# Head and tail of a two-layer decoder kernel: input rows loaded ahead of constants and page tables, output rows transposed straight from the residual

## What is computed

```python
def layer_prompt(x, p):
    xn = rmsnorm(x, p['norm1_g'])
    qa, ka, va, logf, glu, qc, kvc, gc, ud, vd = project(xn, pos, p)
    # four mixers: forgetting attention, convolution, sparse attention, gating
    y = merge_and_ffn(x, (o_a, o_b, o_c, o_d), p)   # h = x + o @ w_out;  y = h + relu(norm(h) @ w_ff1)^2 @ w_ff2
```

## Time and profile before

| | us |
|---|---|
| median of 3 runs | 3554.17 (3553.68 to 3555.39) |
| the profiled execution's own time | 3539.97 |
| its span in the trace | 3538.2 |
| TensorE busy in the span | 3287.5 (93%) |
| VectorE busy | 1470.2 (42%) |
| ScalarE busy | 1022.0 (29%) |
| GpSimd busy | 206.4 (6%) |

### The profile page before, as it was taken

One profiled execution on the slowest core, in us unless ns is written; L12 is line 12 of the kernel. 1 busy time (PEld: TensorE's weight loads), 2 busy tenths in 40 slices (PEclk: granted clock), 3 DMA queues, 4 the chain that ended last, 5 costly groups with the idle time before them and its releaser, 6 DMA issues.

```text
span 3538.2 us, 55597 instructions
## 1 busy us (share of the span) xinstructions
PE 3287.5 (93%) x22450; PEld 1873.5 (53%) x22450; DVE 1470.2 (42%) x2767; ACT 1022.0 (29%) x1814; POOL 206.4 (6%) x136
## 2 busy tenths in 40 slices
PE   5999988888699999999989998888887999999998
PEld 3555566666554444444445555666664444444444
DVE  4875553333544311332168566433336533113321
ACT  2112344444433310231102233444443322012211
POOL 0211110000200000000002111000001000000000
PEclk8999999999899999999999999999998999999999
DMA  6432254142221221123153325334323112111322
GB/s 197 152 103 77 75 167 141 68 144 79 81 92 42 59 60 30 42 59 91 49 145 104 103 77 151 110 91 140 122 62 103 48 48 61 47 35 47 84 73 75
DMA packets 377363, 312.49 MB, mean 88 GB/s; under 512 B 123357, under 2 KB 360314, under 8 KB 370042
## 3 DMA queue, kind: packets, MB, share of 16 engines
q1 hardware_dynamic: 369738, 208.60, 20.9%
q0 software_dynamic: 7424, 101.19, 7.7%
HBM read 264.35 MB, written 50.46 MB: 89 GB/s over the span
## 4 chain that ended last, share of the span: by engine, by line
PE 84%; DVE 6%; ACT 4%; issue 2%; DMA 2%; SPq 1%; POOL 0%; POOLq 0%; DVEq 0%; ACTq 0%
PE PS L938 44%; PE PS L1053 10%; PE PS L1313 5%; PE PS L1336 5%; PE PS L967 4%; PE PS L1204 3%; PE PS L1028 2%; PE PS L1355 1%; PE PS L1386 1%; ACT arena L1620 1%; DVE arena L1904 1%; PE PS L1250 1%; PE PS L1211 1%; DVE arena L2182 1%; PE PS L1103 1%
## 5 line engine op out<-in xcount | busy, mean ns | idle before, releaser
L938 PE MATMUL PS<-arena 128*128 128x512 bf16 (+1 forms) x10080 | 1549.1, 317 | 0.0
L938 PEld LDWEIGHTS PS<-arena 128*128 128x128 bf16 x10080 | 753.5, 98 | 794.6
L1053 PE MATMUL PS<-arena 128*128 128x512 f32 (+3 forms) x1152 | 477.6, 570 | 0.0
L1497 ACT ACTIVATE arena<-arena 128x1024 bf16<-128x1024 f32 (+1 forms) x112 | 145.4, 1300 | 1097.0 <-PE PS L938 1076.9
L2481 DVE TENSOR_TENSOR arena<-PS,arena 128x1088 f32<-128x1088 f32 (+1 forms) x48 | 62.0, 1292 | 654.8 <-PE PS L938 631.2
L1053 PEld LDWEIGHTS PS<-arena 128*128 128x128 f32 (+1 forms) x1152 | 208.6, 184 | 236.3 <-issue 203.3
L2187 DVE TENSOR_REDUCE arena<-PS 128x1 f32<-128x1024 f32 (+5 forms) x192 | 138.9, 724 | 362.3 <-PE PS L1316 361.6
L1313 PE MATMUL PS<-arena 128*128 128x512 f32 (+3 forms) x576 | 231.1, 509 | 8.0 <-ACT arena L1629 8.0
L2505 DVE SCALAR_TENSOR_TENSOR arena<-PS,arena 128x1088 f32<-128x1088 f32 x64 | 82.7, 1292 | 354.7 <-PE PS L938 354.3
L1336 PE MATMUL PS<-arena 128*128 128x64 f32 x1632 | 213.4, 276 | 0.0
L1336 PEld LDWEIGHTS PS<-arena 128*128 128x128 f32 x1632 | 201.1, 195 | 8.2 <-issue 5.2
(11 more groups left out here) (340 smaller groups left out, 2871.1 us busy)
## 6 DMA issues: line engine op xcount, KB each, us to landing
arena<-in_w_ff SPq DMA_DIRECT2D x64, 512.0 KB, 4.1
arena<-in_w_ff SPq DMA_DIRECT2D x32, 1024.0 KB, 5.9
arena<-in_cache_nsa_kv SPq DMA_DIRECT2D x256, 64.0 KB
x_s<-arena SPq DMA_DIRECT2D x24, 544.0 KB, 3.5
arena<-x_s SPq DMA_DIRECT2D x2, 4352.0 KB, 13.0
arena<-in_w_in SPq DMA_DIRECT2D x4, 2048.0 KB, 14.7
arena<-in_w_out SPq DMA_DIRECT2D x16, 512.0 KB, 4.3
arena<-in_w_in SPq DMA_DIRECT2D x12, 512.0 KB, 5.7
```

Source lines behind the costliest of these rows:

```text
L938: last = mm(PS[:, 1536 * k + a:1536 * k + a + wd], ww[:, c, :], xx[:, c, a:a + wd], start=c == 0 and n == 0, stop=c == blocks - 1 and n == 2)
L1053: last = mm(PS[0:r, c * 512:c * 512 + b - a], XNT[:, j, t * P:t * P + r], Wt[:, j, a:b], start=j == 0, stop=j == KD - 1)
L1497: run(WH[k][:, 0:blocks, :], src[k][:, 0:blocks, :], ACT.Copy).then_inc(S["w_hi"], 1)
```

## The change

SyncE now issues the identity alone, then row tiles 0 to 2, then the rest of the constants, then tiles 3 to 8, each into a buffer of its own, with no waits. After them come the page-table loads: `pages`, four loads that write `piece_rows` straight from the page table (one for every fourth partition; `quad_s` is gone), and the 16 of `block_rows`. Gains and gate weights follow, then the wait for the last copy, and the barrier; the eight stores of the residual are issued after the barrier, ahead of the layer's loads. TensorE waits for the identity alone before it starts. VectorE works out the page rows between the sums of tiles 6 and 7. In the tail TensorE transposes straight out of `XT` and uses all eight banks (four tiles), ScalarE copies the first half of each tile and VectorE the second, and each tile has its own buffer `XS`, so that no wait for a store is left before the end.

```diff
-        XS = [lo.take(DM) for _ in range(2)]
-        XO = [lo.take(KD * P, k=KD, n=P) for _ in range(2)]
+        XS = [lo.take(DM) for _ in range(QT + 1)]
...
         def _(sp):
-            sp.dma_start(const, A["consts"]).then_inc(loaded_once, 16)
+            sp.dma_start(const[:, 0:P], A["consts"][:, 0:P]).then_inc(ident_in, 16)
...
+            for t in range(3):
+                row_in(t)
+            sp.dma_start(const[:, P:], A["consts"][:, P:]).then_inc(const_in, 16)
+            for t in range(3, QT + 1):
+                row_in(t)
             sp.dma_start(pages, A["page_table"].rearrange("b j -> (b j)").unsqueeze(0)).then_inc(loaded_once, 16)
-
+            for r in range(4):
+                sp.dma_start(piece_rows[r:P:4, 0:4], A["page_table"].rearrange("b j -> (b j)").rearrange("(g n) -> n g", g=4)).then_inc(loaded_once, 16)
             for j in range(NPG):
                 r = slice(j * (P // NPG), (j + 1) * (P // NPG))
                 sp.dma_start(block_rows[r, :], A["page_table"][:, j:j + 1].rearrange("b o -> o b").to_broadcast([P // NPG, NB])).then_inc(loaded_once, 16)
-            sp.dma_start(quad_s.unsqueeze(2), A["page_table"].rearrange("b j -> (b j)").unsqueeze(1).to_broadcast([NB * NPG, 4]).unsqueeze(2)).then_inc(quad_out, 16)
-            sp.wait_ge(quad_out, 16)
-            sp.dma_start(piece_rows[:, 0:4], quad_s.rearrange("(g n) r -> (n r) g", g=4)).then_inc(loaded_once, 16)
...
             sp.wait_ge(S["row_ev"], QT + 1)
+            arrive(sp, "sp")
             for n in range(KD):
                 store_residual(n)
-            arrive(sp, "sp")
...
-            pe.wait_ge(loaded_once, 304)
...
+            pe.wait_ge(ident_in, 16)
+            for t in range(QT + 1):
+                k, r = t % 2, rows_of(t)
+                pe.wait_ge(S[f"row_in{t}"], 16)
+                if t >= 2:
                     pe.wait_ge(S["row_ev"], t - 1)
                 for j in range(KD):
                     at = (2 * k + j // 4) * 512 + (j % 4) * P
-                    last = tr(PS[:, at:at + r], XS[k][0:r, j * P:(j + 1) * P], ident[0:r, 0:r])
+                    last = tr(PS[:, at:at + r], XS[t][0:r, j * P:(j + 1) * P], ident[0:r, 0:r])
...
+            pe.wait_ge(const_in, 16)
             arrive(pe, "pe")
...
-            def row_out(t, k, m):
+            for t in range(QT + 1):
                 r = rows_of(t)
-                pe.wait_ge(S["row_cp"], t + 1)
-                if not (isinstance(t, int) and t < 2):
-                    pe.wait_ge(S["row_ev"], t - 1)
+                if t >= 4:
+                    pe.wait_ge(S["row_ev"], t - 3)
+                    pe.wait_ge(S["row_odd"], t - 3)
                 for j in range(KD):
-                    at = (2 * k + j // 4) * 512 + (j % 4) * P
-                    last = tr(PS[0:r, at:at + P], XO[k][:, j, 0:r], ident)
+                    at = (2 * (t % 4) + j // 4) * 512 + (j % 4) * P
+                    last = tr(PS[0:r, at:at + P], XT[:, j, t * P:t * P + r], ident)
...
-                if not (isinstance(t, int) and t < 2):
-                    act.wait_ge(S[f"row_out{k}"], 16 * m)
-                run(XS[k][0:r, 0:512], PS[0:r, 1024 * k:1024 * k + 512], ACT.Copy)
-                run(XS[k][0:r, 512:1024], PS[0:r, 1024 * k + 512:1024 * k + 1024], ACT.Copy).then_inc(S["row_ev"], 1)
...
+                run(XS[t][0:r, 0:512], PS[0:r, at:at + 512], ACT.Copy).then_inc(S["row_ev"], 1)
...
-            dve.wait_ge(loaded_once, 304)
+            dve.wait_ge(ident_in, 16)
+            dve.wait_ge(const_in, 16)
...
+            def page_rows():
+
+                dve.wait_ge(loaded_once, 336)
...
+            for t in range(QT + 1):
+                if t == QT - 1:
+                    page_rows()
+                row_squares(t, t % 2, t // 2)
             arrive(dve, "dve")
...
-            def row_cp(t, k, m):
-                r = rows_of(t)
-                if not (isinstance(t, int) and t < 2):
-                    dve.wait_ge(S["row_T"], t - 1)
-                V.tensor_copy(XO[k][:, :, 0:r], XT[:, :, cols(t)]).then_inc(S["row_cp"], 1)
...
+            for t in range(QT + 1):
+                r, at = rows_of(t), t % 4 * 1024 + 512
+                dve.wait_ge(S["row_T"], t + 1)
+                V.tensor_copy(XS[t][0:r, 512:DM], PS[0:r, at:at + 512]).then_inc(S["row_odd"], 1)
...
-            pool.wait_ge(loaded_once, 304)
+            pool.wait_ge(loaded_once, 336)
```

More of the change, by code:

```diff
@@ L172, in build_step @@
         y_s = scratch("y_s", (P, 2 * ROWS))
-        quad_s = nc.dram_tensor("quad_s", (NB * NPG, 4), I32).ap()
         x_s = scratch("x_s", (P, KD * ROWS))
@@ L428, in build_step @@
         loaded_once = sem("loaded_once")
-        quad_out = sem("quad_out")
+        ident_in = sem("ident_in")
+        const_in = sem("const_in")
         names("act_done dve_done")
-        names("col_inv col_mean col_rstd row_mean row_rstd row_in0 row_in1 row_T row_ev row_out0 row_out1 row_cp")
+        names("col_inv col_mean col_rstd row_mean row_rstd row_in0 row_in1 row_in2 row_in3 row_in4 row_in5 row_in6 row_in7 row_in8 row_T row_ev row_odd row_out")
         names("sq_ready sq_added sq_summed xn_ready xt_free w_tok gains glu_mm glu_ev glu_in glu_sig glu_done")
@@ L436, in build_step @@
         names("x_in head_in v_in0 v_in1 gate_in kv4_in fox_ready sl_in snb_in rank_ready rank_out q_in aux_in ocb_in os_out oc_ready sm_ready ce2 dmx dex ee_ready wt_ready vb_ready s_mm nm_ready p_ready pt_T pt_evA pt_evD pv_mm o_done cs_ready ce_ready cp_ready o_ready o_out pad_ready")
[L437 removed]
+        names("od_in oh_in gn_in yb_in wo_in od_norm ss_ready h3_sq oa_hi u_hi oa_ready oa_T oa_ev y_hi")
         names("g2_in xh_ready xl_ready w_in0 w_in1 w_hi w_lo g_mm g_ev u_ready")
@@ L510, in arrive @@
             e.sem_clear(go[who])
[L512 to L533, removed]
         SUMS_OF = {3: [(1, 0), (1, 1)], 4: [(1, 2), (2, 0)], 5: [(2, 1), (2, 2)], 6: [(3, 0), (3, 1)], 7: [(3, 2)]}
@@ L589, in _, with row_in @@
         def _(sp):
-            sp.dma_start(const, A["consts"]).then_inc(loaded_once, 16)
+            sp.dma_start(const[:, 0:P], A["consts"][:, 0:P]).then_inc(ident_in, 16)
+            def row_in(t):
+                src = A["x_prompt"][0, t * P:(t + 1) * P, :] if t < QT else A["x_sample"].rearrange("b t d -> (b t) d")
+                sp.dma_start(XS[t][0:P if t < QT else NS, :], src).then_inc(S[f"row_in{t}"], 16)
+            for t in range(3):
[3 more added lines that the diff above has]
+                row_in(t)
             sp.dma_start(pages, A["page_table"].rearrange("b j -> (b j)").unsqueeze(0)).then_inc(loaded_once, 16)
+            for r in range(4):
+                sp.dma_start(piece_rows[r:P:4, 0:4], A["page_table"].rearrange("b j -> (b j)").rearrange("(g n) -> n g", g=4)).then_inc(loaded_once, 16)
             for j in range(NPG):
@@ L620, in _ @@
             first = slice(0, 1)
-            over_tiles(sp, row_in, between={5: lambda: (norm_in(first), gates_in(0, first))})
-            gates_in(1, first)
+            norm_in(first)
+            for f in range(2):
+                gates_in(f, first)
             def store_residual(n):
@@ L881, in _ @@
                 arrive(sp, "sp")
-            def row_out(t, k, m):
+            for t in range(QT + 1):
+                dst = O["y_prompt"][0, t * P:(t + 1) * P, :] if t < QT else O["y_sample"].rearrange("b t d -> (b t) d")
                 sp.wait_ge(S["row_ev"], t + 1)
[L886 to L893, removed]
+                sp.wait_ge(S["row_odd"], t + 1)
+                sp.dma_start(dst, XS[t][0:P if t < QT else NS, :]).then_inc(S["row_out"], 16)
             for f in range(2):
@@ L897, in _ @@
             sp.wait_ge(x_out, 128 * (layers + 1))
-            sp.wait_ge(S["row_out0"], 16 * 5)
-            sp.wait_ge(S["row_out1"], 16 * 4)
+            sp.wait_ge(S["row_out"], 16 * (QT + 1))
         @block.tensor
@@ L1787, in _ @@
                 arrive(act, "act")
-            def row_out(t, k, m):
-                r = rows_of(t)
+            for t in range(QT + 1):
+                r, at = rows_of(t), t % 4 * 1024
                 act.wait_ge(S["row_T"], t + 1)
-                if not (isinstance(t, int) and t < 2):
-                    act.wait_ge(S[f"row_out{k}"], 16 * m)
-                run(XS[k][0:r, 0:512], PS[0:r, 1024 * k:1024 * k + 512], ACT.Copy)
-                run(XS[k][0:r, 512:1024], PS[0:r, 1024 * k + 512:1024 * k + 1024], ACT.Copy).then_inc(S["row_ev"], 1)
-            over_tiles(act, row_out)
+                run(XS[t][0:r, 0:512], PS[0:r, at:at + 512], ACT.Copy).then_inc(S["row_ev"], 1)
         @block.vector
@@ L1814, in _ @@
             V.tensor_copy(wnegb, C("wneg"))
[L1815 to L1830, removed]
             def add_square(n, total, parts, times=0):
@@ L1842, in row_squares @@
                 V.reduce_sum(SQA[:, cols(t)], SQT[k][:, :, 0:rows_of(t)].rearrange("p k n -> p n k"), AX).then_inc(S["sq_added"], 1)
-            each_tile(row_squares)
```

(32 more changed lines are left out.)

13 lines of the change are left out of this document (removed).

## The result

| | before | changed |
|---|---|---|
| median of 4 runs, us | 3553.93 (3548.72 to 3555.39) | 3524.92 (3523.57 to 3525.53) |
| ratio | | 0.9911, 95% interval 0.9898 to 0.9924 |
| own time of the traced execution | 3539.97 | 3523.57 |
| its span | 3538.2 | 3521.8 |
| start to first instruction behind the first barrier | 57.24 | 31.15 |

The medians differ by 29.0 us, the forecast was 32.4; the ratio of 0.9911 stands for 31.6 us, and its interval for 27 to 36. The two traces differ by only 16.4. The head gives 26.1 and the tail 4.9; between the barriers, where the programs do the same work, the trace after is 14.6 longer.

The account below looks back on a forecast made before the run. TensorE carries 84% of the chain and layer instructions stay, so only head and tail can win: 25.7 + 6.7 - 0 = 32.4 us off 3554.2 gives 3521.8 us, range 3513 to 3533.

Parts of the forecast that it names:

- the offset: Whole kernel: median of runs lies 14.2 us above the profiled execution, for no known reason; carried over to the changed kernel.
- Input and tiles: Head: tile 0 lands at 5.3, tile 3 at 13.5; ScalarE paces at 2.07 per tile; TensorE starts the layer at 31.5.
- one cause of ScalarE's gap: Head: tile 3 lands only behind the constants, at 13.5, so its copy starts at 15.5, two us lost.
- Page loads: Head: last in line, issued by 22.5, landing 2.3 later at 24.8, 0.8 before VectorE wants them.
- Rival 1: Head: page loads become the wait and VectorE ends 5 us later, 3526.8; chance 0.09.
- Moved stores: Layer 0: eight stores issued behind the barrier shift SyncE's later issues by 8.0 us; cost set at 0.
- The mixing weights, which I called tight: Layer 0: loads land at 135 to 138, VectorE reads them at 135.47; a wait of 0 to 2.5 us.
- Rival 2: Layer 0: SyncE's queue takes back at most 8.0 us of the gain, 3529.8; chance 0.08.
- Tail: After the last barrier: first store at 3518.0, stores then bound, end at 3531.5 for 3538.2, 6.7 us less.
- My bound for a slow drain: Tail: if stores drained at 246 GB/s, the gain would be 2 us less.
- Rival 3: Head: input at 246 GB/s instead of 405, tile 3's data 6.2 us longer, 3528.0; chance 0.07.
- Rival 4: Start of the layer: TensorE's clock stays at 2.4 GHz after the barrier, 2.5 us less, 3519.3; chance 0.05.

Follow-up runs that it names:

- casts_late: Changed kernel with VectorE's wait for the constants and its three casts moved into the page rows; first instruction behind the barrier at 30.50, own time 3516.97 us.
- gp_pages2: Changed kernel with page rows computed by GpSimd and VectorE's casts behind its sum of tile 4; median 3518.0 us, ratio 0.9905 to the kernel before.
- both_late: Changed kernel with constants loaded behind tile 8 and VectorE's wait and casts moved into the page rows; barrier passed at 31.36, own time 3528.83 us.

## Why the prediction was right

The measured median, 3524.9, is 3.1 above the 3521.8 forecast and inside the range. The head's mechanism was right in the main; two of its steps came out by luck, and so did the offset. By its steps:

**Input and tiles.** Tile 0 at 5.34 (5.3), tile 3 at 13.2 (13.5), last copy 26.3 (26.5), VectorE's end 29.85 (30.1), TensorE 31.15 (31.5). The rate of 405 GB/s taken from the stores of the earlier trace rows held for the loads. I had one cause of ScalarE's gap and there were two. I had written that the casts "now lie before tile 0"; they lie at 12.0, behind the constants, and hold VectorE's first sum. The size came out right by luck: the bound that I had left out puts tile 3's copy at 15.36, within 0.2 us of the one that I had. Mine holds only as long as the clock is at the 1.2 GHz level when tile 3 comes; in casts_late it was not, and the tile took 1.1 instead of the 1.97 that I had kept for all tiles. For the first tile, whose eight transposes took 1.97 in both traces, the profile's clock column shows 1.00, not the 0.50 that goes with this speed elsewhere; no row explains that.

**Page loads.** They landed at 24.9 (measured in casts_late and gp_pages2; by 25.56 in the changed kernel), as forecast (24.8), but by three errors that cancel. SyncE was not held by the full queue: it had issued the last row load by 6.57, not 14. The 21 small issues took 14.4 us instead of 8.4, 0.68 each instead of 0.4, and were through by 20.97, not 22.5. And the last of them landed not 2.3 behind the issues but some 4.5 (20.44 to 24.9 in casts_late). Rival 1 (they become the wait) did not come in the changed kernel, by less than 0.7 us, but does in casts_late (0.18) and both_late (2.19).

**Moved stores.** The shift was 8.5 us behind the barrier (8.0 forecast). The mixing weights, which I called tight, did not hold VectorE; the 0.9 us wait is one that I had not listed, for `xt_free`. Their worth before the barrier was about 3.3, since without them VectorE is last. Rival 2 did not come.

**Tail.** 17.9 us against 16.1: this is the term that was mis-sized, 4.9 instead of 6.7. First store 3506.69, 2.8 behind the barrier (2.6 forecast); drained 15 us behind it (15.3). Then 2.9 us pass from the end of the flow to the end of the span, where I had put 0.8. The 2.9 us of the old last store, `out_y_sample`, issue to end less transfer, were there to be read, and I counted part of them as latency hidden by the queue. Nothing hides it for the last one. My bound for a slow drain was off as well: at 246 GB/s the 9.75 us of stores would take 16, and the tail would gain about 0.4, not 2. The stores moved at 406, so nothing came of that.

**Input rate.** Rival 3 did not come: tile 3 landed as computed from 405 GB/s. The rule of the Trainium skill, page "DMA: Bandwidth & Descriptors", section Bandwidth, that transfers want 1 MiB for 75% of peak, does not bind loads of 512 KB that are queued back to back here: from 14 to 16 us, with the constants landed and row tiles 4 and on still to land, the queue moved 410 GB/s. (What it calls descriptor-dominated are transfers under 64 KB, not of 64 KB as I had it; nothing rested on that.)

**The clock behind the barrier.** Rival 4 did not come: the squares' six products took 4.07 us as before, at a granted clock of 0.50.

**Offset.** I carried 14.2 us over without a reason; that it was right is luck. The reason is that the trace of before on record is the shortest between the barriers of all twelve taken, with the least time at the lower clock, and its 3539.97 lies 7.2 below the fastest of all other runs of that kernel (3547.16). Taking the traces alone would have given 3507.6 for the changed kernel, and it was never that fast (3510.91 at best).

## What to carry to other kernels

Behind a barrier that waits for everyone, moving one engine's work out pays only down to the next to arrive: here 8 us of stores were worth 3.3, and 2.5 us of ScalarE nothing, since the page loads were next; taking the page rows and casts off VectorE's path gave 2.4. Count the small transfers issued last as the ones that arrive last, and put down the end of the last store in full, 2.9 us here before and after. And before reading a gain of one per cent out of two traces, take a second trace of the old kernel.

## What the runs showed of the hardware

- Equal instructions took 3458 to 3478 us between the same two barriers, with TensorE busy 3261 to 3280 us for them, as 134 to 170 us of them passed at the 1.2 GHz level (eight traces with all matmul records; the four others have 3467 to 3471); VectorE and ScalarE moved by 1.5 us at most.
- Small page-table issues cost SyncE 0.40 us each ahead of the row loads and 0.68 each behind them, 21 in 14.4 us, and the last landed some 4.5 us behind its issue; the eight 512 KB row loads and the constants between them were issued in 0.43 to 0.58 each, without being held.
- GpSimd did the page rows' ten small instructions in 2.5 us, VectorE in 1.6.
